# A two-layer streaming encoder step in split fp32: first stages reordered, low parts read last, and the order of norms, weight splits and down tiles moved

## The chip, the cores and the metric

The kernel runs on one core of a Trainium2 chip. The metric is the device time of one execution in microseconds (us). TensorE multiplies, ScalarE (ACT in the rows), VectorE (DVE) and GpSimd (POOL) do elementwise work, each from its own instruction stream, and SyncE (SP) issues most DMAs. The streams are synchronised by semaphores that the kernel writes out by hand.

## The reference

```python
def reference(x_prompt, x_sample, state_conv, cache_k, cache_v, ...):
    for i in range(2):
        hp, hs = rms_norm(xp, g_mix[i]), rms_norm(xs, g_mix[i])
        if i == 0:      # conformer convolution
            gp = conv_glu_in(hp, w_pw1[0], b_pw1[0])        # a * sigmoid(gate), 1024 -> 2 x 1024
            ...         # 31-tap depthwise conv, LayerNorm, silu, pointwise w_pw2
        else:           # 16 heads, 4 kv heads, window of own and 2 previous chunks of 64
            qp, kp, vp = qkv_proj(hp, w_qkv[0], qn_g[0], kn_g[0])
            mp = swa_prompt(qp, kp, vp, sinks[0], w_o[0])
            ...
        xp = xp + mp
        xp = xp + swiglu_ffn(rms_norm(xp, g_ffn[i]), w_gate[i], w_up[i], w_down[i])   # 2816 wide
        ...             # the same for xs
```
`xp` has 1024 rows and `xs` 32, of 1024 channels each. All data are float32.

## The kernel before

The residual `x` stays in SBUF for the whole step, channels on partitions (8 blocks of 128), tokens along the free dimension. The tokens are two halves: A is the first 512, B the other 512 and the 32 sample rows (544). A half is worked through a stage as a whole, then the other.

Every float32 product is made of three in the faster fp32r format. An operand is split into a high part, which ScalarE writes with a Copy into an fp32r tile, and a low part, the rest. A weight of 128x1024 comes by DMA into `raw`, ScalarE's `hi()` (L857) copies it to `whi`, GpSimd's `lo()` (L1909) subtracts to `wlo`. There are two buffers of each, used in turn; a program-wide list of tiles (`tags`) fixes which weight is n-th. For weight n, `hi()` waits for the DMA and, through `whi_free`, for the last product that reads `whi` of weight n-2; `lo()` waits for `hi()` and for the end of weight n-2's tile. The normalised half is split too, into `hAh` and `hAl` (or `hBh`, `hBl`): ScalarE writes the high part of a block of 128 channels, then VectorE the low part (`low`, L1406).

`proj` (L346, L355) makes one output tile of 128 channels: for each of 8 blocks high x high and high weight x low half, then `mid`, other TensorE work put between, then low weight x high half. A tile of the A half is 24 products of 512 columns in one PSUM bank, one of the B half 48 products of 272 columns in two banks. `take` hands out banks in two rings of four and makes TensorE wait until the last user of a bank has given it back.

The order of the work is written out by hand for each engine. First, x is transposed, its rows' factors are found by ScalarE, and A is normalised by products with diagonals (L427). `SEQ1` is then the order of 29 tiles of the first pointwise product (`g` is the gate, `a` the value). Each place in it is a slot, and ScalarE, VectorE and GpSimd have their share of the A half's convolution in each. Of 31 taps, VectorE adds most up in PSUM (`conv`, L1508), and `NP` of them ScalarE multiplies (`taps`, L987) and GpSimd adds (L1940). Then come the channel mean (L364), the mean of squares (L381), the norm `lnA`, the second pointwise product, and so on.

A feed-forward stage `ffn(l, h)` has 11 groups. Group G makes gate and up tiles of two blocks (b = 0 to 3) and then `down` (L560, L567) of group G-1: 8 output tiles d, of which the first four read one weight buffer (u = 0) and the last four the other (u = 1). VectorE's `add_to_x` (L1592) adds each to `x` and frees its bank. Six weights belong to a group, and `hi()` runs ahead of them: the four calls in b = 0 to 3 make those of b = 2, b = 3 and of `down`'s two halves, the fifth and sixth those of the next group's b = 0 and b = 1.

In the stages `ffn(0, "B")` and `ffn(1, "A")` the attention of the other half runs in the same groups. In group G VectorE reads the scores of four units of G-1 (`read_scores`), ScalarE takes their exps (`exps`, L1100), VectorE the reciprocals of their sums (`denominators`, L1656), ScalarE scales them (`scale_probs`, L1112). Group G+1 turns them and multiplies by the values, which ScalarE and VectorE split (`out_high`, L1069; `out_low`, L1680). `act_high` (L1059) and `act_low` (L1604) split the activation for the next group's `down`. VectorE's part behind the tiles of b is this:

```python
for d in range(KD):
    if G:
        add_to_x(("D", l, h, G - 1, d))
    if d == 1:
        read_scores(att, cur, 3)
    if d == 2:
        out_low(att, prev, 3)
    if d == 3:
        act_low(l, h, G, 1)
    if G and d % 2:
        denominators(att, cur, d // 2)
```

Of the kernel before, what the change touches and what calls it, by code (L numbers as in the profile page):

```python
# [38 lines left out]
NP = {"A": 10, "B": 10}  # L39
# [22 lines left out]

def conv_a_steps():

    done, glu, out = 0, 0, []
    for s in range(len(SEQ1)):
        if s and SEQ1[s - 1][:2] == ("a", "A"):
            glu += 1
        want = 0 if s < 2 else 1 if s in (5, 6) else 6 if s < 5 else 7
        new = KD * NQ["A"] if s == len(SEQ1) - 1 else done + want  # L70
        new = min(new, glu * NQ["A"])
        out.append((done, new))
        done = new
# [19 lines left out]
def products(h, j):  # L93

    return min(KD * NP[h], NP[h] * (j + 5) // NQ[h]) if j else 0

# [8 lines left out]
def build(nc, a, outs):  # L105
    y_prompt, y_sample, conv_prompt, conv_sample, k_prompt, v_prompt, k_sample, v_sample = outs
    with ExitStack() as ctx:
# [88 lines left out]
        late_in = sem("late_in")  # L196
        params_in, sinks_in, copied = sem("params_in"), sem("sinks_in"), sem("copied")
# [9 lines left out]
        row_sq, row_rs, diag_ready = sem("row_sq"), sem("row_rs"), sem("diag_ready")  # L207
# [25 lines left out]

        last_tile = {}
        w_need = {}
# [56 lines left out]
        def _(pe):  # L292
            user, used, to_free, nxt = [None] * 8, [0] * 8, [0] * 8, [0, 0]
# [3 lines left out]
            def take(key, h, ring=0):  # L297
                b = nxt[ring]
                if h == "B" and b % 2:
                    b += 1  # L300
                b %= 4
                w = CH[h]
                nxt[ring] = (b + w) % 4
                b += 4 * ring
# [32 lines left out]
            def proj(h, key, ev, n, last=True, mid=None):  # L337
                take(key, h)
                out = parts(key)
                pe.wait_ge(w_hi, n + 1)  # L340
                for k in range(KD):
                    if ev:
                        wait_h(h, ev, k)
                    for src in (hi_[h], lo_[h]):
                        for o, c0, w in out:
                            ins = nc.tensor.matmul(o, whi[n % 2][:, P * k:P * (k + 1)], src[:, k, c0:c0 + w],  # L346
                                                   start=(k == 0 and src is hi_[h]), stop=False)
                if last:
                    ins.then_inc(whi_free, 1)
# [3 lines left out]
                for k in range(KD):  # L353
                    for o, c0, w in out:
                        ins = nc.tensor.matmul(o, wlo[n % 2][:, P * k:P * (k + 1)], hi_[h][:, k, c0:c0 + w],  # L355
                                               start=False, stop=(k == KD - 1))
# [27 lines left out]
            def row_factors():  # L384

                b = take(("mean", "mix0B"), "B")
                for t in range(4, 9):
                    pe.wait_ge(diag_ready, t + 1)
# [5 lines left out]
            def x_group(q):  # L394
                t, half = q // 2, q % 2
                w = P if t < 8 else TS
                b = take(("xt", q), "A", int(q >= 8))
# [8 lines left out]
            pe.wait_ge(consts, 9)  # L406
            for q in range(8):
                x_group(q)
                if q == 5:
                    pe.wait_ge(params_in, 16 * 7)  # L410
                    b = take(("par", 0), "A", 1)
                    nc.tensor.transpose(ps[:, b, 0:40], R[0:40, 0:P], ident[0:40, 0:40])
                    for z in range(2):
                        ins = nc.tensor.transpose(ps[:, b, P + 120 * z:P + 120 * (z + 1)],
                                                  R[0:120, P * (3 + z):P * (4 + z)], ident[0:120, 0:120])
                    ins.then_inc(pfull[b], 1)
                    b = take(("par", 1), "A", 1)
                    for z in range(2):
                        ins = nc.tensor.transpose(ps[:, b, 124 * z:124 * (z + 1)], R[0:124, P * (1 + z):P * (2 + z)],
                                                  ident[0:124, 0:124])  # L420
                    ins.then_inc(pfull[b], 1)
# [1670 lines left out]
```

## Time and profile before

| | |
|---|---|
| median of 3 runs | 2288.69 us (2288.39 to 2290.41) |
| profiled execution, its own time | 2286.99 us |
| its span | 2285.2 us |
| busy share PE, PEld, DVE, ACT, POOL | 98%, 88%, 49%, 45%, 49% |
| granted TensorE clock, mean | 0.988 of full |
| HBM read, written | 184.39 MB, 5.10 MB |

The span runs from the first to the last instruction. PE is TensorE's products, PEld its weight loads. The chain of work that ended last lies on TensorE for 91% of the span. In a row of the timeline stand the start, the length, engine, line, operation, what is written and read, how many were merged, and in brackets the engine's idle time before it with what ended that.

### The profile page before, as it was taken

Reading aid. Unit: us, or ns where it says so; the run is one execution under the profiler, and the core shown is the slowest. Engines: PE = TensorE matmul, PEld = TensorE weight load, DVE = VectorE, ACT = ScalarE, POOL = GpSimd, SP = SyncE. Lnnn points to the kernel's source line nnn. Section 1 sums busy time; section 2 is a strip of 40 time slices with the busy share of each in tenths; the row PEclk is TensorE's granted clock in tenths of the full one; section 3 lists DMA queues with packets and bytes.
Section 4 is the critical chain, followed back from the end, with each engine's and each line's share of the span. In section 5 each row is a group of like instructions: output and inputs, shape, how many; then the busy total and the mean of one; then the engine's idle time right before and its main releaser. Section 6 shows DMA issues by size and latency. Waiting matters only on the chain.

```text
span 2285.2 us, 34556 instructions
## 1 busy us (share of the span) xinstructions
PE 2228.7 (98%) x13954; PEld 2017.0 (88%) x13954; DVE 1111.8 (49%) x1822; ACT 1037.8 (45%) x1659; POOL 1113.6 (49%) x573
## 2 busy tenths in 40 slices
PE   8998899999999999999999999999999999999999
PEld 7797678887889799999999898888888989999999
DVE  4987668873434544445443535454554142222223
ACT  6544655533524654544552466465655332222222
POOL 3787569975446533333334544333333443443433
PEclk9999899999999999999999999999999999999999
DMA  4111123332333522222222342222222323233222
GB/s 149 47 54 57 57 65 102 97 102 83 94 100 89 104 86 79 75 74 75 75 75 84 93 99 84 83 83 78 80 84 75 92 77 99 93 102 93 84 89 90
DMA packets 313644, 194.15 MB, mean 85 GB/s; under 512 B 40374, under 2 KB 286734, under 8 KB 313486
## 3 DMA queue, kind: packets, MB, share of 16 engines
q1 hardware_dynamic: 311608, 190.83, 28.3%
q8 instruction: 112, 1.84, 0.3%
q10 hardware_dynamic: 1878, 1.11, 0.2%
q14 instruction: 46, 0.38, 0.1%
HBM read 184.39 MB, written 5.10 MB: 83 GB/s over the span
## 4 chain that ended last, share of the span: by engine, by line
PE 91%; POOL 3%; DVE 2%; ACT 2%; issue 1%; DMA 0%; ACTq 0%; DVEq 0%; POOLq 0%
PE ps L346 42%; PE ps L355 21%; PE ps L560 14%; PE ps L567 7%; PE ps L530 2%; POOL accp L1940 2%; PE ps L516 1%; PE ps L364 1%; PE ps L492 1%; PE ps L491 1%; POOL wlo L1909 1%; PE ps L381 1%; DVE x L1592 1%; POOL rs L1919 0%; DVE sq L1401 0%
## 5 line engine op out<-in xcount | busy, mean ns | idle before, releaser
L1909 POOL TENSOR_TENSOR wlo<-raw,whi 128x1024 fp32r<-128x1024 f32 x342 | 838.9, 2453 | 1095.4 <-PE ps L355 763.7
L857 ACT ACTIVATE whi<-raw 128x1024 fp32r<-128x1024 f32 x342 | 361.8, 1058 | 628.4 <-PE ps L346 366.6
L346 PE MATMUL ps<-hBh,whi 128*128 128x272 f32 x2112 | 440.7, 290 | 6.0 <-DVE x L1592 3.2
L346 PE MATMUL ps<-hBl,whi 128*128 128x272 f32 x2112 | 440.0, 290 | 0.0
L346 PE MATMUL ps<-hAh,whi 128*128 128x512 f32 x1056 | 418.7, 397 | 18.5 <-DVE hAl L1406 10.5
L346 PE MATMUL ps<-hAl,whi 128*128 128x512 f32 x1056 | 416.1, 394 | 0.0
L1592 DVE TENSOR_TENSOR x<-ps,x 128x512 f32<-128x512 f32 (+1 forms) x368 | 258.4, 705 | 244.2 <-PE ps L567 181.3
L346 PEld LDWEIGHTS ps<-hBh,whi 128*128 128x128 f32 x2112 | 334.2, 190 | 8.9 <-issue 4.9
L346 PEld LDWEIGHTS ps<-hBl,whi 128*128 128x128 f32 x2112 | 332.4, 189 | 0.0
L355 PE MATMUL ps<-hBh,wlo 128*128 128x272 f32 x2112 | 291.2, 290 | 0.0
L355 PEld LDWEIGHTS ps<-hBh,wlo 128*128 128x128 f32 x2112 | 273.7, 188 | 2.5 <-issue 1.9
L355 PE MATMUL ps<-hAh,wlo 128*128 128x512 f32 x1056 | 270.6, 399 | 2.9 <-POOL wlo L1909 2.9
L346 PEld LDWEIGHTS ps<-hAh,whi 128*128 128x128 f32 x1056 | 200.3, 190 | 68.8 <-DVE hAl L1406 11.1
L1599 DVE TENSOR_TENSOR s<-ps,s 128x512 f32<-128x512 f32 (+1 forms) x88 | 62.3, 708 | 369.3 <-PE ps L355 367.2
L355 PEld LDWEIGHTS ps<-hAh,wlo 128*128 128x128 f32 x1056 | 197.0, 190 | 46.6 <-issue 4.3
L346 PEld LDWEIGHTS ps<-hAl,whi 128*128 128x128 f32 x1056 | 200.9, 190 | 40.8
L1940 POOL TENSOR_TENSOR accp<-accp,prod 128x512 f32<-128x512 f32 (+1 forms) x144 | 199.7, 1387 | 25.2 <-ACT prod L987 12.4
L1665 DVE TENSOR_TENSOR ptl<-ps,pth 128x512 fp32r<-128x512 f32 (+1 forms) x64 | 42.1, 658 | 167.1 <-ACT pth L1088 167.1
L1508 DVE SCALAR_TENSOR_TENSOR ps<-gxB,dwc,ps 128x574 f32<-128x574 f32 x152 | 114.1, 811 | 0.0
L1088 ACT ACTIVATE pth<-ps 128x512 fp32r<-128x512 f32 (+1 forms) x64 | 36.6, 572 | 167.6 <-PE ps L516 167.6
L1508 DVE SCALAR_TENSOR_TENSOR ps<-gxA,dwc,ps 128x512 f32<-128x512 f32 x152 | 101.8, 749 | 0.0
L560 PE MATMUL ps<-act0h,whi 128*128 128x272 f32 (+1 forms) x288 | 78.6, 327 | 4.5 <-DVE x L1592 3.9
(254 smaller groups left out, 3161.7 us busy)
## 6 DMA issues: line engine op xcount, KB each, us to landing
raw<-in_w_gate_dram SPq DMA_DIRECT2D x88, 512.0 KB, 3.8
raw<-in_w_up_dram SPq DMA_DIRECT2D x88, 512.0 KB, 3.8
raw<-in_w_down_dram SPq DMA_DIRECT2D x88, 512.0 KB, 3.6
raw<-in_w_pw_dram SPq DMA_DIRECT2D x38, 512.0 KB, 4.0
raw<-in_w_qkv_dram SPq DMA_DIRECT2D x32, 256.0 KB, 3.7
raw<-in_w_o_dram SPq DMA_DIRECT2D x64, 128.0 KB, 2.9
stage<-in_x_prompt_dram SPq DMA_DIRECT2D x8, 512.0 KB, 5.7
raw<-in_w_qkv_dram SPq DMA_DIRECT2D x8, 512.0 KB, 3.7
```

The lines of the kernel that those rows point to most:

```text
L346: ins = nc.tensor.matmul(o, whi[n % 2][:, P * k:P * (k + 1)], src[:, k, c0:c0 + w], start=(k == 0 and src is hi_[h]), stop=False)
L355: ins = nc.tensor.matmul(o, wlo[n % 2][:, P * k:P * (k + 1)], hi_[h][:, k, c0:c0 + w], start=False, stop=(k == KD - 1))
L530: ins = nc.tensor.matmul(ps[0:HD, 6, 0:256], v[:, slot, HD * g:HD * (g + 1)], p[:, 256 * z:256 * (z + 1)], start=(z == 0 and w == 0), stop ...
L560: ins = nc.tensor.matmul(o, whi[n % 2][:, wc], src[s + e][:, c0:c0 + w], start=(e == 0 and src is ach), stop=False)
L567: ins = nc.tensor.matmul(o, wlo[n % 2][:, wc], ach[s + e][:, c0:c0 + w], start=False, stop=(e == 1))
L857: nc.scalar.activation(whi[n % 2][:], raw[n % 2][:], ACT.Copy).then_inc(w_hi, 1)
L1508: link(nc.vector.scalar_tensor_tensor((X, Y)[q % 2], two(gx[h][:, c, t:t + w]), dwc[:, KD * t + c:KD * t + c + 1], (X, Y)[q % 2], ALU.mult ...
L1592: nc.vector.tensor_tensor(xd, pt(key), xd, ALU.add).then_inc(fr(key), 1)
L1599: nc.vector.tensor_tensor(s, pt(key), s, ALU.mult).then_inc(fr(key), 1)
L1665: nc.vector.tensor_tensor(ptl[:, 0:w], ps[:, 5, 0:w], f(pth[:, 0:w]), ALU.subtract).then_inc(pt_lo, 1)
L1909: nc.gpsimd.tensor_tensor(wlo[n % 2][:], raw[n % 2][:], f(whi[n % 2][:]), ALU.subtract).then_inc(w_lo, 1)
L1940: nc.gpsimd.tensor_tensor(accp[p % 2][:, 0:w], accp[p % 2][:, 0:w], prod[r % 2][:, 0:w], ALU.add).then_inc(padd, 1)
```

## The change

1. `NP["A"]` is 9 instead of 10, so VectorE has 24 steps for a channel block instead of 23. `conv_order` puts the last two steps of a block behind the first six of the next, which uses two other banks. `CONV_A` gives 8 steps to a slot instead of 7.
2. The opening: dummy products (`keep_busy`) before the transposes, before the normalising products and after the squares' mean of `lnA`. The gains come by their own semaphore, the other parameters are transposed later. The normalising products of blocks 2 to 7 stand inside the first tile (`ahead`). The x transposes of B use a ring of two banks. ScalarE writes the diagonals of B and loads the sigmoid table behind them.
3. `proj`: a tile that is the first to read a normalised half (`new`) goes through all high x high products, then low weight x high, then high weight x low. Its `whi` is free only at its end, so that `hi()` two weights later waits for the whole tile.
4. Norms: `factor` loads its table before it waits for the mean; the means of mix1B and ffn1B and some sums of squares of lnB have other places; in the last norm VectorE normalises ahead of its adds. The channel mean of A takes the last block straight from `gx`.
5. `ffn` on ScalarE, stages with attention: the fifth `hi()` of a group stands before `out_high` and `act_high`, the sixth before the last exps.

```diff
-NP = {"A": 10, "B": 10}
+NP = {"A": 9, "B": 10}
...
+def conv_order(h):
+    own = [[(p, q) for q in range(NQ[h])] for p in range(KD)]
+    if h == "B":
+        return sum(own, [])
+    out, ends = [], []
+    for p in range(KD):
+        out += own[p][:6] + ends + own[p][6:-2]
+        ends = own[p][-2:]
+    return out + ends
...
-        want = 0 if s < 2 else 1 if s in (5, 6) else 6 if s < 5 else 7
+        want = 0 if s < 2 else 2 if s in (5, 6) else 6 if s < 5 else 8
...
+def products_a(s):
+    return 0 if s < 2 else min(KD * NP["A"], 2 * (s - 1) if s < 6 else 8 + 3 * (s - 5))
...
+        RINGS = [(0, 4), (4, 4), (6, 2)]
...
+            def whi_done(ins, n):
+                whi_read[n] = len(whi_read) + 1
+                ins.then_inc(whi_free, 1)
...
+                new = ev and waited.get(h, 0) < h_need(ev, KD - 1)
...
                 for k in range(KD):
-                    if ev:
-                        wait_h(h, ev, k)
-                    for src in (hi_[h], lo_[h]):
...
+                    if ahead is not None:
+                        ahead(k)
+                    if k == 0:
+                        pe.wait_ge(w_hi, n + 1)
+                    if new:
+                        pe.wait_ge(h_hi[h], h_need(ev, k))
+                    ins = product(whi, hi_, k, start=(k == 0))
+                    if not new:
+                        ins = product(whi, lo_, k)
+                if not new and last:
+                    whi_done(ins, n)
...
+                if new:
+                    for k in range(KD):
+                        wait_h(h, ev, k)
+                        ins = product(whi, lo_, k, stop=(k == KD - 1))
...
+            def keep_busy(n):
+                for _ in range(n):
+                    nc.tensor.matmul(ps[:, 7, 0:P], ident[:], ones_d[:], start=True, stop=True)
...
+            keep_busy(10)
             for q in range(8):
                 x_group(q)
...
+            keep_busy(14)
+            half_a(0)
+            half_a(1)
...
-            pe.wait_ge(csummed, KD - 1)
-            mean(("lm", "A"), "A", ones_d, csum)
+            b = take(("lm", "A"), "A")
+            pe.wait_ge(csummed, KD - 2)
+            nc.tensor.matmul(ps[:, b, :], ones_d[:], csum[:, 0:512], start=True, stop=False)
+            pe.wait_ge(c_ready, KD)
+            nc.tensor.matmul(ps[:, b, :], ones_d[:], gx["A"][:, ORDER["A"][-1], 0:512], start=False, stop=True
+                             ).then_inc(pfull[b], 1)
             proj("B", ("a", "B", 1), "mix0", load(("a", 1)))
             square_mean("lnA", lambda k: pe.wait_ge(sq_ready, k + 1))
+            keep_busy(24)
...
-                         mid=(lambda: norm_mean("mix1B")) if (h, d) == ("A", 2) else None)
+                         ahead=(lambda k: k or norm_mean("mix1B")) if (h, d) == ("A", 3) else None)
...
-                        down(l, h, G - 1)
-                if (l, h) == (1, "A"):
-                    norm_mean("ffn1B")
+                        down(l, h, G - 1, (lambda: norm_mean("ffn1B")) if (l, h, G) == (1, "A", NG - 1) else None)
...
-                if n >= 2:
-                    act.wait_ge(whi_free, n - 1)
+                if n - 2 in whi_read:
+                    act.wait_ge(whi_free, whi_read[n - 2])
+                elif n >= 2:
+                    full(act, last_tile[n - 2])
...
+                nc.scalar.preload_act_table_set("natural_log_exp_and_others")
                 full(act, key)
...
-                nc.scalar.preload_act_table_set("natural_log_exp_and_others")
...
+                    first = att and G and (l, h, G) != (1, "A", NG - 1)
+                    if first:
+                        hi()
                     if att:
                         out_high(att, prev, 3)
                     act_high(l, h, G, 1, att)
...
                     if att:
                         exps(att, cur, 0)
                         exps(att, cur, 1)
-                    if G:
+                    if G and not first:
                         hi()
                     if att:
                         scale_probs(att, cur, 0)
                         exps(att, cur, 2)
                         scale_probs(att, cur, 1)
+                    if first:
+                        hi()
+                    if att:
                         exps(att, cur, 3)
-                    if G:
+                    if G and not first:
                         hi()
...
                 for d in range(KD):
-                    add_to_x(("D", l, h, NG - 1, d))
                     if (l, h) == (1, "A"):
...
                         norm_parts("ffn1B", C_FFN[1], d, d + 1)
+                    add_to_x(("D", l, h, NG - 1, d))
...
-                            if G == 6:
-                                for k in (2, 3):
-                                    sum_squares("lnB", k)
                         lo()
+                        if (l, h, G) == (0, "A", 6):
+                            for k in (2, 3):
+                                sum_squares("lnB", k)
```

## Rows read from the trace of the kernel before

**Rows 1.** The page, busy time and share of each engine.
```profile
PE 2228.7 (98%) x13954; PEld 2017.0 (88%) x13954; DVE 1111.8 (49%) x1822; ACT 1037.8 (45%) x1659; POOL 1113.6 (49%) x573
```

**Rows 2.** TensorE's waits: what for, us in total, times, longest.
```profile
PE ps L346 <- DVE hAl L1406: 10.5, 6, 7.1
PE ps L364 <- POOL csum L1962: 8.9, 1, 8.9
PE ps L346 <- ACT s L968: 4.8, 1, 4.8
...
PE ps L346 <- DVE x L1592: 4.0, 2, 3.2
PE ps L560 <- DVE x L1592: 3.9, 3, 1.3
PE ps L346 <- ACT qraw L1143: 3.7, 2, 1.9
...
PE ps L355 <- POOL wlo L1909: 2.9, 1, 2.9
```

**Rows 3.** Timeline of ScalarE in one group of the B half's stage.
```profile
949.67 0.38 ACT L1069 ACTIVATE hAh<-ps 64x256 fp32r<-64x256 f32 x1 [1.64 <-PE ps L530]
950.07 0.66 ACT L1059 ACTIVATE act3h<-s 128x544 fp32r<-128x544 f32 x1
950.75 1.28 ACT L1100 ACT_TABLE_LOAD   x1
952.04 0.41 ACT L1100 ACTIVATE sco<-sco,col 128x129 f32<-128x129 f32 x1
...
952.83 0.49 ACT L1100 ACTIVATE sco<-sco,col 128x257 f32<-128x257 f32 x1
...
955.24 1.06 ACT L857 ACTIVATE whi<-raw 128x1024 fp32r<-128x1024 f32 x1 [1.33 <-PE ps L560]
956.21 0.68 ACT L1112 ACTIVATE sco<-sco,col 128x128 f32<-128x128 f32 x2
```

**Rows 4.** Timeline of VectorE and of GpSimd in the same group.
```profile
954.60 0.16 DVE L1656 RECIPROCAL col<-col 128x2 f32<-128x2 f32 x1
954.68 0.70 DVE L1592 TENSOR_TENSOR x<-ps,x 128x544 f32<-128x544 f32 x1
...
956.50 2.85 DVE L1604 TENSOR_TENSOR act3l<-s,act3h 128x544 fp32r<-128x544 f32 x1
...
956.38 2.39 POOL L1909 TENSOR_TENSOR wlo<-raw,whi 128x1024 fp32r<-128x1024 f32 x1 [4.90 <-ACT whi L857]
```

**Rows 5.** Timeline of TensorE in the same group: ends and starts of tiles.
```profile
954.73 0.41 PE L560 MATMUL ps<-act1l,whi 128*128 128x272 f32 x2
...
955.64 0.49 PE L560 MATMUL ps<-act0h,whi 128*128 128x272 f32 x2
...
960.20 0.49 PE L560 MATMUL ps<-act0h,whi 128*128 128x272 f32 x2 [1.31 <-DVE x L1592]
```

**Rows 6.** Timeline of one group of layer 1's A half: ScalarE, VectorE, TensorE.
```profile
1528.98 1.06 ACT L857 ACTIVATE whi<-raw 128x1024 fp32r<-128x1024 f32 x1 [0.73 <-PE ps L560]
...
1528.57 0.67 DVE L1592 TENSOR_TENSOR x<-ps,x 128x512 f32<-128x512 f32 x1
...
1527.80 0.40 PE L560 MATMUL ps<-act0h,whi 128*128 128x512 f32 x1
```

**Rows 7.** Stretches: us, PE, PEld, DVE, ACT, POOL busy, granted clock, DMA.
```profile
83.12:205.27 122.15, 122.15 (x817) 114.27 (x815) 110.08 (x176) 62.00 (x86) 108.62 (x77) 1.00 0.17 50
...
214.00:219.00 5.00, 4.84 (x17) 3.81 (x18) 2.66 (x5) 1.94 (x4) 2.41 (x2) 0.55 0.25 74
536.60:546.60 10.00, 7.12 (x26) 5.46 (x25) 3.21 (x5) 3.26 (x5) 8.38 (x5) 0.83 0.19 52
767.90:773.20 5.30, 5.26 (x16) 4.22 (x17) 2.14 (x4) 0.53 (x2) 0.65 (x1) 0.68 1.08 187
1348.90:1353.00 4.10, 4.06 (x32) 4.09 (x33) 2.01 (x3) 1.09 (x4) 0.76 (x1) 1.00 0.99 206
```

More of the change, by code:

```diff
@@ L60, with joined @@
 GLU = [(h, c) for w, h, c in SEQ1 if w == "a"]
+def conv_order(h):
[7 more added lines that the diff above has]
+    return out + ends
+CONV = {h: conv_order(h) for h in "AB"}
+def joined(h, j):
+    return sum(q == NQ[h] - 1 for _, q in CONV[h][:j])
 def conv_a_steps():
@@ L297, in take @@
             def take(key, h, ring=0):
+                first, size = RINGS[ring]
                 b = nxt[ring]
@@ L353, in proj @@
                 for k in range(KD):
-                    for o, c0, w in out:
-                        ins = nc.tensor.matmul(o, wlo[n % 2][:, P * k:P * (k + 1)], hi_[h][:, k, c0:c0 + w],
-                                               start=False, stop=(k == KD - 1))
+                    ins = product(wlo, hi_, k, stop=(not new and k == KD - 1))
+                if new:
+                    for k in range(KD):
+                        wait_h(h, ev, k)
+                        ins = product(whi, lo_, k, stop=(k == KD - 1))
                 ins.then_inc(pfull[place[key][0]], 1)
@@ L396, in x_group @@
                 w = P if t < 8 else TS
-                b = take(("xt", q), "A", int(q >= 8))
+                b = take(("xt", q), "A", 2 if q >= 8 else 0)
                 if half == 0:
@@ L542, in values, with down @@
                 ins.then_inc(pv_full, 1)
-            def down(l, h, G):
+            def down(l, h, G, between=None):
                 stage_ft = FT * (2 * l + (h == "B"))
@@ L547, in down @@
                 for u in range(2):
+                    if u and between is not None:
+                        between()
                     n = load(("D", l, G, u))
@@ L971, in _, with taps @@
             done = {"A": 0, "B": 0}
-            def taps(h, j):
-                for i in range(done[h], products(h, j)):
+            def taps(h, n):
+                for i in range(done[h], n):
                     p, c, t, r = in_order(h, i)
@@ L1002, in _ @@
                     row_factor(4, 9)
+                    act.wait_ge(row_rs, 4)
+                    nc.scalar.activation(rsc[:, 4:9], rsc[:, 4:9], ACT.Copy, scale=float(D)).then_inc(row_rs, 1)
+                    act.wait_ge(row_rs, 5)
+                    for t in range(4, 9):
+                        w = P if t < 8 else TS
+                        nc.scalar.activation(diag[0:w, t, 0:w], ident[0:w, 0:w], ACT.Copy, scale=rsc[0:w, t:t + 1]
+                                             ).then_inc(diag_b, 1)
+                    nc.scalar.preload_act_table_set("sigmoid_and_others")
                 if s == 5:
@@ L1415, in norm_parts, with x_copy @@
                         low(ev[-1], ev[:-1], k)
-            for q in range(8):
+            def x_copy(q):
                 full(dve, ("xt", q))
@@ L1447, in late_params @@
             def late_params():
+                full(dve, ("par", 1))
+                b = place["par", 1][0]
+                nc.vector.tensor_copy(stc[:], ps[:, b, 248:488])
+                nc.vector.tensor_copy(dwc[:], ps[:, b, 0:TAPS * KD]).then_inc(fr(("par", 1)), 1)
                 full(dve, ("par", 2))
@@ L1498, in conv @@
                             freed(dve, ("par", 1))
[L1499 to L1502 removed]
+                        if h == "A" and p < 2:
+                            for key in before_conv[2 * p:2 * p + 2]:
+                                freed(dve, key)
+                    if q == (0 if h == "A" else 1) and pos:
+                        dve.wait_ge(c_ready, pos - 1 if h == "A" else pos)
                     if q < 2:
@@ L1929, in _, with taps @@
             summed = {"A": 0, "B": 0}
-            def taps(h, j):
-                for i in range(done[h], products(h, j)):
+            def taps(h, n):
+                for i in range(done[h], n):
                     p, c, t, r = in_order(h, i)
```

178 lines of the change are left out of this document (90 added, 88 removed).

## The prediction

> **What bounds the kernel now.** I read the page's busy shares first: TensorE is busy 98% of the span [rows 1], so nothing can win much: the idle time, 2285.2 - 2228.7 = 56 us over the whole span, and some half-rate clock. It can lose more, by making TensorE wait where it doesn't now. The list of TensorE's waits shows where the idle time lies [rows 2]: 10.5 us for the low parts of a normalised half, 8.9 us for the last channel sum of the convolution, 4.8 us for a sigmoid, 2.9 us for one weight low part, and small ones for PSUM banks that VectorE's adds or ScalarE's copies give back. None lies in the two long attention-and-feed-forward stages but three gaps of 1.3 us. Last I read those stages engine by engine, since the change moves a waiting instruction there: ScalarE [rows 3, 6], VectorE and GpSimd [rows 4], TensorE [rows 5, 6]. What the reader is to see there: inside `down` of the B half TensorE fills two pairs of banks in turn, so tile d starts only after VectorE's `add_to_x` of tile d-2. Tile 4 starts at 955.64, right behind the add of tile 2 (954.68 + 0.70) [rows 4, 5]. That add stands on VectorE behind the reciprocal at 954.60, which waits for `exps(0)` on ScalarE. So the chain ScalarE exps, VectorE reciprocal, VectorE add, TensorE tile has no slack already.
>
> **The step that decides: the early `hi()`.** Of the six weight copies in a group the fifth is that for the next group's first tile. It reuses the buffer that `down`'s first half reads, so it waits for that half's last hi/lo product whatever its place: 954.73 + 0.41 = 955.14, and the copy starts at 955.24 [rows 3, 5]. Before, `out_high`, `act_high`, a table load and four exps ran ahead of it, from 949.67 to 953.8. The change puts it ahead of them all (`first`). It can't start earlier, and what stands behind it on ScalarE now waits from 948 to 955. That ScalarE lets nothing pass is in the rows: the probabilities' scaling had its reciprocal at 954.76, but ran at 956.21, after the copy [rows 3, 4]. The Trainium skill ("TensorE: Matmul & The Clock Gate", "Architectural detail: the array is 16× 32×32, not 1× 128×128") says of ScalarE and VectorE that their queues are strictly first in, first out; by a queue that could pass, the step would cost nothing (the first rival), and the row sides with the page.
>
> New chain in the B-half stage, from the copy's start: copy 0.97, `out_high` 0.40, `act_high` 0.68, table load 1.29, first exps 0.79 and its read 0.1 [rows 3]: 955.24 + 4.2 = 959.5. Reciprocal 0.08, add 0.70: 960.3; TensorE picks up 0.2 later, 960.5 instead of 955.64 [rows 4, 5]. That is 4.8 us for each group with scores to turn, which are groups 1 to 8. Three of these groups have today a gap of 1.3 us (1.4 with its restart), because `act_low` took 2.85 us beside GpSimd's weight split [rows 2, 4, 5]. There `act_low` now comes at 961.4, after that split has ended (956.38 + 2.39), and I take the gap as gone. 5 x 4.8 + 3 x 3.4 = 34 us. The Trainium skill ("SBUF — State Buffer", "SBUF: two separate sides") says that VectorE with two SBUF inputs and GpSimd exclude each other for a whole instruction; this agrees with the 2.85 us. If the gap stayed all the same, the sum would be 4 us higher. Groups 9 and 10 have no scores, but `out_low` and `act_low` still wait for the late `out_high` and `act_high`: about 1.5 us each (0 if VectorE catches up, 3 if `act_low` meets the split), 3 us. So 37 us in this stage.
>
> In the A-half stage of layer 1 a tile takes one bank of four, so tile 6 is the one that needs the add of tile 2. Copy at 1528.98 [rows 6], + 0.97 + 0.40 + 0.65 + 1.29 + 1.0 (two exps of 0.49) = 1533.3, add until 1534.0, TensorE at 1534.2. Tile 3 starts at 1527.80 and a tile takes 1.39, so tile 6 was due at 1532.0: 2.2 us, in groups 1 to 9: 20 us.
>
> **What the stalls do to the clock.** After the gap of 2.88 us 10 us ran at a granted 0.83, after that of 1.89 us 5.3 us at 0.68, each 1.7 us of full clock lost; after 1.79 us it stayed at 1.00 [rows 7] (half rate is 1.2 GHz, full 2.4). A gap of 4.8 us in otherwise dense work should cost it each time: 8 x 1.6 = 13 us. Gaps of 2.2 us lie between the row that fell and those around it; I take two in three, 9 x 2/3 x 1.6 = 10 us. Bounds for both together: 0 and 27.
>
> **What it wins.** First stages: the ends of `conv` are spread (8 steps a slot instead of 7, so that the last slot has 2 instead of 17), the last channel goes straight to TensorE, and the wait of 8.9 us should fall to some 1.5. The 4.8 us wait for the sigmoid falls to about 1: three products fewer stand ahead, and its table (1.29 us) is loaded before. Half rate around 214 us (5 us at 0.55) gives back 2.2 and that after the sigmoid's wait 1.5 [rows 2, 7]. The opening, where the first tile is threaded between the normalising products, wins some 3 us, but x transposes on two banks instead of four then wait for ScalarE, about 1.5 to 2 back. Against it, VectorE: it was busy 110.1 of 122.2 us [rows 7], and 20 more steps of 0.67 make it 123.5, so it lags by 1 to 3 us. Extra dummy products cost 0 to 2 (ahead of the diagonals, else in idle time). Together 15 us, bounds 5 and 20. For these dummy products no row of before exists; the nearest are the normalising ones.
>
> Low parts last: at lnA the first hi comes 2 us earlier (table loads moved), but TensorE is then idle most of the time until the eighth, so its remaining 16 products may run at half rate: 1 us won, bounds -1.5 and 3. ffn0A the same way 1 (bounds 0 and 3). The other norms had no such wait; there the copy for the next but one tile waits for the whole tile, 2 us later, covered by a tile of 5.4 or 6 us. lnB: `sum_squares` 2 and 3 move behind the weight split that TensorE waited 2.9 us for; with 1.4 of clock 4.3. ffn0B and ffn1A: table load ahead of the wait, 1.3 each of the two `qraw` waits of 1.89 and 1.79, and 1.7 of clock: 4.3. mix1B's mean one tile later 1.5. ffn1B: mean half a `down` earlier, norm ahead of the adds, lows last: the 3.2 us wait becomes about 1, and the tile gets denser: 4 (bounds 2 and 5). Sum of gains 15 + 1 + 1 + 4.3 + 4.3 + 1.5 + 4 = 31.
>
> **Sum.** 37 + 20 + 13 + 10 - 31 = +49 us. The profiled execution took 2286.99 us (span 2285.2 and 1.8 around it), 1.7 below the median of the runs; so 2336 in the profile and about 2337 as a median. I state 2337.
>
> **Rivals.** (1) Faster: the moved copy costs nothing, as it would if ScalarE's work behind it were not needed before 961. For it: ScalarE waits for TensorE for that copy today too. Against it: tile 4's start at 955.64 hangs on the exps. It decides if the first exps of a group end within 0.2 us of today's 952.9. Then only the gains are left: 2257; with a stall under 1 us a group still faster. Chance 0.12. (2) The stalls come, but the clock doesn't fall for them: + 57 - 31, 2314. For it: the gap of 1.79 us. Against it: the 1.89 and the 2.88. Chance 0.18. (3) VectorE becomes the bound of the first convolution, the dummy products and low clock eat the rest there, and the first stages win under 5 us: 2347. For it: 123.5 us of work in 122.2. Against it: TensorE's banks allow a lag of one tile. Chance 0.12. (4) No net change, stalls half as long and just paid by the gains: 0.02. My forecast: 0.56.
>
> **Numbers.** Measured noise of this kernel is about 0.2% (4.6 us). Faster 0.12, same 0.02, slower 0.86. The range takes in forecast, (2) and (3) with the bounds of the gains and of the clock: 2300 to 2354; it leaves out (1) and (4) and a little on the far side.
>
> **What would show it.** In the profile after: ScalarE's copy of a group standing before `act_high` and waiting some 7 us for TensorE; TensorE waits at `down` for VectorE's add, 8 of 4 to 5 us and 9 of about 2, and the clock under 1 behind them. In the first 220 us: the channel-mean product at about 201 instead of 214, VectorE near full. If ScalarE's exps still end before `down`'s fourth tile, the main step is wrong; if the gaps are there and the clock row stays at 1.00, (2) holds.

## The result, and the profile after

The kernel after takes 2352.73 us (median of four runs, 2351.52 to 2355.49), the one before, on the same chip, 2288.89 (2288.39 to 2290.41): ratio 1.0279, 95% interval 1.0262 to 1.0297, or 64 us slower. 2337 was predicted, with a range to 2354. The profiled execution of after took 2355.49 us (span 2353.6), 2.8 above its median. It has a stretch of half rate near 30 us, and its first 230 us took 3.3 us longer than those of the first experiment, whose order is the same there and whose profile has no such stretch.

TensorE's waits of after (what for, us in total, times, longest), to be held against [rows 2]:
```profile
PE ps L640 <- DVE x L1686: 60.1, 21, 5.0
PE ps L387 <- issue: 8.8, 2, 4.5
PE ps L387 <- ACT hAh L988: 4.6, 6, 1.0
PE ps L387 <- ACT s L1050: 4.0, 2, 3.2
PE ps L387 <- ACT hAh L975: 3.1, 3, 1.5
PE ps L387 <- ACT qraw L1234: 3.1, 2, 1.7
```
One row has taken over: TensorE in `down` waits 60.1 us, 21 times, for VectorE's `add_to_x` (L1686), where it was 3.9 us in 3. The waits for the channel sum (8.9) and for a weight's low part (2.9) are gone. Two of 4.5 and 4.3 us "issue" are new, before the first tile of the B half in the first convolution and in the last norm; both are taken up below. The second was 3.2 us before and then had the name `DVE x`.

The same group of the B half's stage as in [rows 3 to 5], ScalarE, VectorE, TensorE:
```profile
957.19 1.06 ACT L937 ACTIVATE whi<-raw 128x1024 fp32r<-128x1024 f32 x1 [7.21 <-PE ps L640]
958.27 0.38 ACT L1160 ACTIVATE hAh<-ps 64x256 fp32r<-64x256 f32 x1
958.67 0.66 ACT L1150 ACTIVATE act3h<-s 128x544 fp32r<-128x544 f32 x1
959.35 1.28 ACT L1191 ACT_TABLE_LOAD   x1
960.64 0.40 ACT L1191 ACTIVATE sco<-sco,col 128x129 f32<-128x129 f32 x1
...
961.55 0.17 DVE L1750 RECIPROCAL col<-col 128x2 f32<-128x2 f32 x1 [4.92 <-ACT sco L1191]
961.63 0.70 DVE L1686 TENSOR_TENSOR x<-ps,x 128x544 f32<-128x544 f32 x1
...
963.46 0.71 DVE L1698 TENSOR_TENSOR act3l<-s,act3h 128x544 fp32r<-128x544 f32 x1
...
957.18 0.41 PE L647 MATMUL ps<-act1h,wlo 128*128 128x272 f32 x2
962.60 0.79 PE L640 MATMUL ps<-act0h,whi 128*128 128x272 f32 x2 [5.00 <-DVE x L1686]
```
Read it downwards: the copy stands first and waits 7.21 us for TensorE's last read of the old weight. Everything else of ScalarE follows it, the exps end where the reciprocal can start at 961.55, the add follows, and TensorE, which had nothing more to do at 957.6, goes on at 962.60. From copy to reciprocal it is 4.36 us. `act_low` takes 0.71 where it took 2.85 beside the weight split.

A group of layer 1's A half, for [rows 6]:
```profile
1531.88 1.06 ACT L937 ACTIVATE whi<-raw 128x1024 fp32r<-128x1024 f32 x1 [6.60 <-PE ps L640]
...
1536.25 0.67 DVE L1686 TENSOR_TENSOR x<-ps,x 128x512 f32<-128x512 f32 x1
...
1536.97 0.50 PE L640 MATMUL ps<-act2h,whi 128*128 128x512 f32 x1 [1.96 <-DVE x L1686]
```

Stretches of after (columns as in [rows 7]): the first convolution, the two norms of A, lnB's first tile, a feed-forward tile that waited for `qraw`, the products behind one stall of each stage, and behind the gap of the last norm:
```profile
83.00:206.00 123.00, 120.57 (x784) 112.94 (x785) 122.03 (x193) 62.03 (x87) 109.09 (x78) 0.97 0.17 47
226.00:248.00 22.00, 17.37 (x73) 12.81 (x73) 12.54 (x19) 14.68 (x21) 0.90 (x1) 0.77 0.00 1
300.00:316.00 16.00, 12.89 (x53) 9.76 (x53) 15.80 (x25) 7.64 (x12) 5.37 (x4) 0.79 0.22 62
536.00:546.00 10.00, 10.00 (x46) 8.29 (x45) 1.56 (x2) 5.27 (x8) 9.71 (x7) 1.00 0.21 60
757.00:762.00 5.00, 3.32 (x15) 2.42 (x14) 2.14 (x4) 2.73 (x6) 2.37 (x1) 1.00 1.08 210
961.30:968.30 7.00, 5.70 (x25) 5.74 (x26) 3.37 (x7) 3.68 (x14) 0.00 (x0) 0.52 0.28 77
1538.40:1541.90 3.50, 3.50 (x10) 2.68 (x10) 2.65 (x7) 2.79 (x9) 0.34 (x1) 0.51 0.02 7
1941.00:1945.00 4.00, 3.74 (x17) 3.77 (x18) 3.91 (x7) 2.26 (x3) 0.14 (x1) 0.57 0.00 0
```
VectorE is now busy 122.03 of 123 us in the first convolution (110.08 of 122.15 before), and behind a stall of 5.0 us, as behind one of 1.96, TensorE runs near half of its 2.4 GHz.

To see where the time goes, the start of one and the same TensorE product is read in both traces, and their distances are subtracted. For the norms that product is the start of the third tile behind them. The -5.3 of the first stages holds the 3.3 us of the half rate near 30 us. The right column does this for the first experiment, which takes the early copies out:

| stretch, ends at | predicted | after - before | first experiment - before |
|---|---|---|---|
| first stages (squares' mean, 223.15 before) | -15 | -5.3 | -8.6 |
| lnA | -1 | +0.5 | +0.2 |
| ffn0A | -1 | +0.9 | +0.8 |
| lnB | -4.3 | -4.7 | -4.7 |
| ffn0B, ffn1A, mix1B (tables, mean) | -5.8 | -2.4 | -2.2 |
| early copies, B half's stage | +50 | +51.5 | 0 |
| early copies, A half's stage | +30 | +27 | 0 |
| last norm (ffn1B) | -4 | +0.9 | +0.7 |
| sum | +49 | +68.4 | -13.8 |

### The profile page after: what moved, and what is told of

It reads as the page before. It is cut to its first block, busy times and chain, and to the rows that moved or that the text cites. A ratio compares the mean times of both kernels' runs of the same rounds, so it can differ in the third digit from the quotient of the medians.

```text
span 2353.6 us, 34735 instructions
## 1 busy us (share of the span) xinstructions
PE 2258.1 (96%) x14052; PEld 2043.4 (87%) x14052; DVE 1112.4 (47%) x1825; ACT 1032.2 (44%) x1657; POOL 1100.0 (47%) x564
## 4 chain that ended last, share of the span: by engine, by line
PE 91%; ACT 5%; DVE 3%; issue 1%; POOL 0%; DVEq 0%; ACTq 0%; POOLq 0%
PE ps L387 64%; PE ps L640 14%; PE ps L647 6%; PE ps L608 2%; PE ps L594 1%; PE ps L419 1%; ACT L1191 1%; ACT whi L937 1%; ACT sco L1191 1%; DVE x L1686 1%; PE ps L569 1%; PE ps L570 1%; PE ps L436 1%; DVE sq L1498 1%; PE ps L464 0%
## 5 line engine op out<-in xcount | busy, mean ns | idle before, releaser
L387 PE MATMUL ps<-hBh,whi 128*128 128x272 f32 x2112 | 435.4, 290 | 11.1 <-issue 8.8
L387 PE MATMUL ps<-hBl,whi 128*128 128x272 f32 x2112 | 432.3, 289 | 0.0
L387 PE MATMUL ps<-hAh,whi 128*128 128x512 f32 x1056 | 416.4, 397 | 13.8 <-ACT hAh L988 4.6
L387 PE MATMUL ps<-hAl,whi 128*128 128x512 f32 x1056 | 409.8, 394 | 0.0
L1686 DVE TENSOR_TENSOR x<-ps,x 128x512 f32<-128x512 f32 (+1 forms) x368 | 257.2, 704 | 244.7 <-PE ps L647 185.9
L387 PEld LDWEIGHTS ps<-hAl,whi 128*128 128x128 f32 x1056 | 201.0, 190 | 42.3
L2034 POOL TENSOR_TENSOR accp<-accp,prod 128x574 f32<-128x574 f32 (+1 forms) x136 | 189.9, 1397 | 31.3 <-ACT prod L1069 19.9
L1605 DVE SCALAR_TENSOR_TENSOR ps<-gxA,dwc,ps 128x512 f32<-128x512 f32 x160 | 107.2, 748 | 0.0
L1179 ACT ACTIVATE pth<-ps 128x512 fp32r<-128x512 f32 (+1 forms) x64 | 36.6, 572 | 156.0 <-PE ps L594 156.0
```

What stands on the lines that cost most here:

```text
L387: ins = nc.tensor.matmul(o, wt[n % 2][:, P * k:P * (k + 1)], src[h][:, k, c0:c0 + w], start=start, stop=stop)
L1605: link(nc.vector.scalar_tensor_tensor((X, Y)[q % 2], two(gx[h][:, c, t:t + w]), dwc[:, KD * t + c:KD * t + c + 1], (X, Y)[q % 2], ALU.mult ...
L1686: nc.vector.tensor_tensor(xd, pt(key), xd, ALU.add).then_inc(fr(key), 1)
L2034: nc.gpsimd.tensor_tensor(accp[p % 2][:, 0:w], accp[p % 2][:, 0:w], prod[r % 2][:, 0:w], ALU.add).then_inc(padd, 1)
```

## The experiments

### Is it the moved copies, and which of them

The first kernel puts both early `hi()` back and keeps all the rest of the change; the second does the opposite, the kernel before with the early copies alone; the third has only the sixth copy early.
```diff
-                    first = att and G and (l, h, G) != (1, "A", NG - 1)
-                    if first:
-                        hi()
...
-                    if G and not first:
+                    if G:
                         hi()
                     if att:
                         scale_probs(att, cur, 0)
```


> The changed kernel with the fifth and sixth weight copies of a group back in their old places, all else as changed. Theory (the early fifth copy costs both attention stages): the 51.5 and 28.8 us that the two stages lost come back, so about 2272 us, faster than before by some 16 us, with no gap over 2 us at down in these stages. Rival (the longer stages come from the low parts read last or from a buffer that is freed later): 2300 us or more, and gaps remain.

Measured: 2274.03 us (2272.88 to 2275.84), ratio 0.9934, interval 0.9919 to 0.9949. TensorE's wait in `down` is back at its old size:
```profile
PE ps L387 <- issue: 8.8, 2, 4.4
PE ps L387 <- ACT hAh L988: 4.6, 6, 1.0
PE ps L640 <- DVE x L1681: 4.6, 4, 1.3
PE ps L387 <- ACT s L1050: 4.0, 2, 3.2
```


> The kernel before with only the two copies moved ahead. Theory: eight gaps of 4.7 to 5.0 us in the B half's stage, nine of 1.7 to 2.2 us in the A half's, half-rate clock behind them, together about 80 us: 2369 us. Rival (the stalls need the other edits too): under 2330 us.

Measured: 2368.93 us, ratio 1.0343, interval 1.0326 to 1.0361; the wait for the add is 59.6 us in 20 times.

> The changed kernel with the fifth copy back in its place and the sixth still ahead of the last exps. Theory (the fifth alone does it): within 5 us of the kernel with both back, about 2272 us. Rival (both share the loss, since the last exps then wait for the end of down): 2290 to 2320 us.

Measured: 2276.69 us, ratio 0.9944, interval 0.9929 to 0.9959. The profile has none of the stalls.

So the change is two things that hardly touch each other: the early copies cost 2352.7 - 2274.0 = 78.7 us on top of the rest, and 3.4%, about 79, on top of the kernel before; the rest wins 15.3, against the kernel before run beside it (2289.30). Of the copies it is the fifth. The sixth, put before the last exps, reads 2.7 us more, with overlapping intervals.

### What part of a stall is clock

Eighteen dummy products for TensorE before the second half of `down`, in the B half's stage of after, for each of its eight long stalls (`G` in the edit is that of `down`, 0 to 7, so these are groups 1 to 8). They stand where TensorE has nothing to do, and write to a bank that nobody reads.
```diff
                     if u and between is not None:
                         between()
+                    if u and (l, h) == (0, "B") and G <= 7:
+                        keep_busy(18)
```


> The changed kernel with 18 dummy products (3.9 us at full rate) put into each of the eight waits of 4.7 to 5.0 us in the B half's stage; results unchanged. Theory (the wait costs twice, once as idle time and once as half rate behind it): the clock stays at full, and 8 x 1.6 = 13 us come back: about 2340 us. Rival (behind the wait VectorE's adds pace the tiles, so the half rate costs nothing): 2350 us or more.

Measured: 2340.93 us, ratio 1.0225, interval 1.021 to 1.024: 11.8 us less than after. The same group in its trace, TensorE (the row of the dummies counts two records for each):
```profile
953.65 4.18 PE L464 MATMUL ps<-ones_d,ident 128*128 128x128 f32 x36
958.82 0.49 PE L642 MATMUL ps<-act0h,whi 128*128 128x272 f32 x2 [0.99 <-DVE x L1688]
959.15 0.41 PE L642 MATMUL ps<-act0l,whi 128*128 128x272 f32 x2
```
The add still comes when it came, so the stall is as long; but two products behind it take 0.41 us at once, where in after the next ones took 0.66. This is the clock's share, apart from that of the wait. From trace to trace the stage is 14.4 us shorter than in after, and 37.1 us longer than before; after's own profiled run lay 2.8 above its median, so the medians show 11.8.

The change's own dummy products (`keep_busy(10)`, `(14)`, `(24)`) removed from the first experiment:
```diff
-            keep_busy(10)
...
-            keep_busy(14)
...
-            keep_busy(24)
```


> The changed kernel with the copies back and without any of the 48 dummy products. Theory (they warm the clock for the opening's transposes, but their 14 in the middle delay the normalising products by about 1 us, and the 24 at lnA only move the half-rate stretch): within 3 us of 2274 us. Rival (they keep the clock where it counts): 2278 us or more.

Measured: 2273.71 us (2272.09 to 2277.98), ratio 0.9934, interval 0.9921 to 0.9948, so no difference to 2274.03.

### Where the gains of the first stages went

All kernels from here on have the copies back. The first puts the normalising products of blocks 2 to 7 into the other ring, because the second tile had stood 3.2 us for the first one's sigmoid:
```diff
-                b = take(("xn", k), "A", 1 - k % 2)
+                b = take(("xn", k), "A", 1 - k % 2 if k < 2 else 1)
```


> The changed kernel with the copies back, and the normalising products that stand inside the first tile take banks of the other ring, so that the second tile no longer takes the first tile's bank and doesn't wait for its sigmoid. Theory (the opening's gain was lost to this bank): the wait of 3.2 us before the second tile goes, 1 to 2 of it come back as a later wait for the x transposes' copies, so about 2 us faster than with the copies back alone, some 2272 us. Rival (VectorE sets when the first B tile's pair is done, whatever the opening): no change there, 2274 us.

Measured: 2271.73 us (2269.97 to 2272.18), ratio 0.9921, interval 0.9907 to 0.9934, 2.3 us less. The wait for the first sigmoid is gone; a wait of 1.3 us for ScalarE's copy of an x transpose has come at 33.7 us, as the theory had it.

Then every tile takes its blocks in pairs, high and low, as before the change, instead of the lows last:
```diff
-                new = ev and waited.get(h, 0) < h_need(ev, KD - 1)
+                new = False
...
-                    if new:
-                        pe.wait_ge(h_hi[h], h_need(ev, k))
+                    if ev:
+                        wait_h(h, ev, k)
```


> The changed kernel with the copies back, and no tile takes the low parts last: each block waits for its low part and takes high and low in pairs, as before. Theory (after the last high part comes TensorE still has two thirds of the tile to do, at half rate, so reading lows last wins next to nothing): within 3 us of 2274 us, half-rate stretches of the same length at lnA. Rival (lows last wins 1 to 2 us at each of lnA, ffn0A and ffn1B): 2277 to 2280 us.

Measured: 2267.56 us, ratio 0.9903, interval 0.9889 to 0.9916: 6.5 us less than 2274.03. Neither theory had it; the lows-last order, taken for a small gain, costs. Stretches of the first experiment (lnA's and ffn0A's first tiles), then of this one:
```profile
220.00:245.00 25.00, 20.36 (x89) 14.90 (x88) 13.11 (x20) 16.32 (x23) 1.48 (x1) 0.80 0.04 12
290.00:312.00 22.00, 19.02 (x96) 15.14 (x95) 19.02 (x27) 11.19 (x16) 7.35 (x5) 0.84 0.13 38
```
```profile
220.00:245.00 25.00, 21.35 (x95) 15.68 (x95) 15.96 (x24) 18.79 (x26) 5.91 (x4) 0.86 0.08 22
290.00:312.00 22.00, 19.38 (x101) 15.56 (x100) 19.23 (x27) 14.64 (x20) 10.76 (x7) 1.00 0.16 48
```
Both the number of products left and their clock differ. Lows last, TensorE does eight single products, at lnA 1.4 us apart as ScalarE brings the blocks, and then sixteen at once, most of them at half rate; in pairs the second product of a block fills part of each wait and fewer are left. From the start of the last block's first product to the end of the tile there are 17 products against 10, a difference of 1.6 us at full rate; it is 6.4 us against 4.1 at lnA and 5.9 against 2.4 at ffn0A, where no half rate is left with pairs. From start of lnA's first tile to that of its third it is 20.9 us with the lows last (226.71 to 247.57) and 19.3 in pairs (224.33 to 243.64); in ffn0A 17.4 (299.13 to 316.53) and 14.7 (295.20 to 309.91), of which 1.4 is given back in the groups behind. The opening gives 1.8, since a low-last tile frees `whi` only at its end and the copy, a table load and the sigmoid come behind that (the second tile's wait is 0.8 us with pairs, 3.2 without); the first convolution gives 0.6 and layer 1 1.8.

Both together:

> The copies back, every tile taking its blocks high and low in pairs, and the normalising products of blocks 2 to 7 in the other ring of banks. Paired alone had brought 2267.6 and the other ring alone 2271.7, against 2274.0 with neither. Theory: the ring removes the second tile's wait for the first one's sigmoid and the pairing what the late low parts cost at lnA, ffn0A and the two qkv halves, so they add up, but both take from the wait before the second tile (3.2 us, 0.8 left with the pairing), so their sum of 8.7 loses about 1: 2266, and no half rate before 80 us. Rival: the time from the second tile to the first B tile is set by VectorE, and what the ring gives is waited for again before the first B tile: within 1 of 2267.6.

Measured: 2267.14 us (2266.04 to 2268.15), ratio 0.9903, interval 0.9886 to 0.9919. The rival: the first B tile starts 1.3 us sooner than with the pairing alone (79.56 for 80.90), and at lnA only 0.75 us are left of it.

In all these kernels TensorE stands 4.4 us before its first B tile. The row says "issue", so the profile names no releaser; the bank that the tile takes is that of A's fourth gate tile, whose sigmoid in after ran from 84.66 to 85.33, behind ScalarE's high parts of the norm of B and three convolution products, and TensorE went on at 85.43. This kernel puts that sigmoid into ScalarE's idle time behind the fifth high part:
```diff
                     for k in range(4 * (s - 5), 4 * (s - 4)):
                         n_hi_part("mix0B", k)
+                        if k == 4:
+                            sigmoid(sig)
+                            sig += 1
```


> The kernel before it (i) with ScalarE's sigmoid of the fourth gate tile of A put behind the fifth high part of the norm of B, in idle time, instead of behind the eighth and three convolution products. Theory: the 4.4 us that TensorE stands before its first B tile are a wait for the bank which that sigmoid frees; with it early the low parts of B (the last at about 80.8 in the kernel with the copies back) are only needed at 81, so the gap falls under 1 and its half-rate stretch goes: 5 to 6 us less than i, about 2260. Rival: VectorE is the bound of the whole stretch; TensorE then waits elsewhere before 210 us, for a bank of a gate or value tile, and i's time stays within 1.5 us.

Measured: 2266.15 us (2265.47 to 2266.81), ratio 0.9897, interval 0.9882 to 0.9912: within 1 us of the kernel without it. TensorE starts its first B tile without a wait, and then:
```profile
85.82 0.82 PE L387 MATMUL ps<-hBh,whi 128*128 128x272 f32 x2 [4.26 <-DVE gxA L1566]
```
The wait has moved by one tile and now carries its real name: VectorE's value tile. That is the rival, VectorE as the bound.

Last, four of VectorE's convolution steps moved out of the two slots in which it also normalises B (with the sooner last norm of the next section):
```diff
-        want = 0 if s < 2 else 2 if s in (5, 6) else 6 if s < 5 else 8
+        want = 0 if s < 2 or s in (5, 6) else 6 if s < 5 else 8
```


> Kernel k and the sooner last norm of m together, and VectorE's four convolution steps of the two slots in which it also normalises B (slots 5 and 6, two each) moved to the slots behind them, with 8 in each as before and fewer left for the last. In k the gap of 4.3 us had only moved to the second B tile, where it was a wait for VectorE's value tile (gxA), with VectorE busy without a break before it. Theory: VectorE is the bound only in the slots with the norm; four steps of 0.68 us less there bring that value 2.7 us earlier, the gap falls to 1.6 and its half-rate stretch of 3.4 us (1.7 of full clock) goes: 4 us less, with 1 from m 2261 to 2262. Rival: VectorE is the bound of the whole convolution (121 us busy of 125); the four steps are then waited for at the channel mean near 203 us, 2 to 3 us, and the time is within 1 of 2265.

Measured: 2263.78 us (2263.10 to 2264.93), ratio 0.9886, interval 0.987 to 0.9903, the fastest of all. TensorE, two places of its trace, and the stretch:
```profile
84.36 0.52 PE L387 MATMUL ps<-hBh,whi 128*128 128x272 f32 x2 [1.86 <-DVE gxA L1568]
...
204.03 1.12 PE L530 MATMUL ps<-gxA,ones_d 128*128 128x512 f32 x2 [2.11 <-DVE gxA L1619]
...
80.00:205.00 125.00, 121.02 (x793) 111.57 (x793) 122.86 (x195) 60.99 (x85) 110.61 (x78) 1.00 0.18 52
```
Both theories are half right. The gap fell by 2.4 us as expected and its half rate went. But the steps taken away are asked for at the channel mean: 2.11 us that weren't there. VectorE, 122.86 of 125 us busy, is the bound of the whole stretch. The two waits together fell from 4.26 to 3.97 us and the squares' mean came 1.2 us sooner than in the kernel before this one, so what was won there is mostly the clock.

### The last norm

The old order of ffn1B in the first experiment (mean behind the whole `down` of group 9, adds ahead of the norm):
```diff
-                        norm_parts("ffn1B", C_FFN[1], d, d + 1)
                     add_to_x(("D", l, h, NG - 1, d))
+                    if (l, h) == (1, "A"):
...
+                        norm_parts("ffn1B", C_FFN[1], d, d + 1)
```


> The changed kernel with the copies back and the last norm (ffn1B) as before: mean behind the ninth down, adds ahead of the norm's steps; lows still last. Theory (the new order keeps back the add that frees the first B tile's banks, so an earlier mean wins nothing): the wait before the first B tile is shorter than 4.3 us, about 3, and from the start of the tenth group's downs to the third B tile no more than 42.3 us pass. Rival (the new order wins, but less than the 4 us of the forecast): over 43 us pass.

Measured, a single run: 2278.59 us. From the start of `down` of group 9 to the third B tile it is 43.65 us, not 42.3 or less; 42.03 in the first experiment, 41.35 before. TensorE:
```profile
1860.75 1.85 PE L387 MATMUL ps<-hBh,whi 128*128 128x272 f32 x12 [3.00 <-issue]
1864.83 0.52 PE L387 MATMUL ps<-hBh,whi 128*128 128x272 f32 x2 [2.23 <-ACT hBh L977]
1866.12 0.59 PE L387 MATMUL ps<-hBh,whi 128*128 128x272 f32 x2 [0.77 <-ACT hBh L977]
```
So the old order needs the pairs to be good; with the lows last the tile runs into the high parts. The fourth case is in the kernel with pairs and the new order: 42.24 us. With pairs the old order is 0.9 us better than the new, with the lows last 1.6 worse.

The other way, in the kernel with both (2267.14): VectorE normalises two blocks between the ninth group's last adds, where it idles 0.7 us each time.
```diff
                         if G:
                             add_to_x(("D", l, h, G - 1, d))
+                        if (l, h, G) == (1, "A", NG - 1) and d in (5, 6):
+                            ...
+                            x_norm("ffn1B", d - 5, C_FFN[1])
```


> Kernel i with the last norm begun sooner: VectorE normalises its first two blocks between the last three adds of the ninth group's down, where it idles 0.7 us before each add, instead of behind them all. Theory: the gap of 4.3 us before the first B tile of the last stage is a wait for the bank that VectorE's sixth add frees, and that add is late because all eight blocks of the norm stand in between; two products of 0.78 us taken out ahead, one of which had met GpSimd's weight split and taken 2.2, bring the add 1.5 to 3 us earlier: 2 to 3 us less than i. Rival: the norm's own length beside the two splits decides wherever it begins, or the low parts are then the last wait: within 1 us of i.

Measured: 2266.38 us (2266.08 to 2267.06), ratio 0.9898, interval 0.9884 to 0.9913: the rival, within 1 us. TensorE still waits 4.36 us. VectorE in its trace:
```profile
1838.37 2.71 DVE L1502 TENSOR_TENSOR hBl<-sq,hBh 128x544 fp32r<-128x544 f32 x1
...
1845.63 2.73 DVE L1497 SCALAR_TENSOR_TENSOR sq<-x,col,rs 128x544 f32<-128x544 f32 x1
...
1851.02 0.68 DVE L1685 TENSOR_TENSOR x<-ps,x 128x512 f32<-128x512 f32 x1
```
One instruction of the norm meets each of GpSimd's two weight splits and takes 2.7 us for 0.75, whichever comes then; the add that frees the bank, the last row, ends at 1851.7, 0.1 before TensorE goes on.

## Why the prediction was right where it was, and where not

**The deciding step held.** Copy, `out_high`, `act_high`, table, exps, reciprocal: predicted 4.2 us from copy to reciprocal, 4.36 measured. The eight stalls were 4.5 to 5.0 us (38.4 together), groups 9 and 10 added 2.7, and the three old gaps of 1.3 are gone, as the 2.85 us of `act_low` are: 38.4 + 2.7 - 3.9 = 37.2 against 37. The A half's nine stalls were 1.7 to 2.2 us, 18.3 together for 20. That it is this step is shown, from both sides, by the first two experiments. The range held by little: 2352.73 lies 1.3 us under its upper end, with gains half as large as forecast and that of ffn1B outside its own bounds. That the time stayed inside was luck in part.

**The clock.** In the B half's stage 51.5 - 37.2 = 14.3 us are left for it, 13 were predicted, and the dummies in the stall won 14.4 of the stage: with them it costs 37.1 us over before, about the waits alone. In the A half's stage 27 - 18.3 = 8.7, against 10. Here not six but four of nine stalls were followed by half rate, 3.4 us each. Held against before group by group, each stall cost 0.27 us more than its idle time even where the clock stayed at 1.00, and those four a further 1.6 each: 9 x 0.27 + 4 x 1.6 = 8.8. The prediction had the clock alone. Where the 0.27 comes from no run shows.

**The first stages: 15 predicted, 5.3 and 8.6 measured.** This is one of the mis-sized terms. 3.3 us lie between the two measured values, those of the half rate near 30 us. Its parts: the wait for the channel sum went wholly (8.9, more than assumed) and the sigmoid's fell from 4.8 to 0.8, as forecast. But "the opening wins some 3 us" was wrong. The threaded products take their banks behind the first tile, so the second tile gets the first one's bank and stands 3.2 us for its sigmoid. And "it lags by 1 to 3 us" for VectorE was too small at one place: it also normalises B there, one step of that took 2.92 us beside a weight split, and the first B tile stood 4.4 us and TensorE's clock fell to half for 3.4 to 6.8 us. So the channel mean's product came at 210.1 us (206.8 in the first experiment) and not near 201. Rival (3) had the mechanism: VectorE is the bound of this stretch. The last experiments showed it, by a wait that moved from the bank to the value tile and then to the channel mean. Its price was near too, under 5 us of gain; that the time came out above its 2347 as well is due to the next points.

**Low parts last: +1 +1 and part of 4 predicted, a loss of about 6.5 in all.** This is a gain with the wrong sign. The prediction saw that "its remaining 16 products may run at half rate" and still took a gain. It had asked when the first product can start. What counts is how many products are left when the last block arrives, and at which clock they run. The experiment with pairs showed it, against both of its own expectations. With pairs the stages do win over before, 1.3 us at lnA and 0.7 at ffn0A with its groups, close to the 1 + 1 that was put down to the lows. The prediction had also taken the later copy at the other norms for "covered by a tile of 5.4 or 6 us"; it named no cost in the opening and in layer 1, and 1.8 us lie in each.

**ffn1B: a gain of 4 predicted, a loss of 0.9.** "The 3.2 us wait becomes about 1" looked to the norm and the low parts. TensorE already waited for a bank before, the one that the sixth add frees; VectorE in before:
```profile
1870.96 0.68 DVE L1592 TENSOR_TENSOR x<-ps,x 128x512 f32<-128x512 f32 x1
```
This add ends at 1871.64, and TensorE goes on at 1871.74. The new order puts six blocks of the norm ahead of that add instead of five, and two of its instructions meet splits (2.23 and 2.70 us); the bank is waited for 4.3 us.

**Tables and means.** lnB won 4.7 (4.3 predicted). The two `qraw` waits fell by 0.2 and 0.4 us only, not 1.3 each; the half rate behind the first of them went, as forecast. ScalarE in the trace of before, then of after:
```profile
762.93 1.06 ACT L857 ACTIVATE whi<-raw 128x1024 fp32r<-128x1024 f32 x1 [1.41 <-PE ps L346]
764.22 1.28 ACT L881 ACT_TABLE_LOAD   x1 [0.23 <-PE ps L364]
```
```profile
754.47 1.06 ACT L937 ACTIVATE whi<-raw 128x1024 fp32r<-128x1024 f32 x1 [1.41 <-PE ps L387]
755.54 1.28 ACT L956 ACT_TABLE_LOAD   x1
```
The load stood behind a weight copy that itself waits for TensorE, and had waited only 0.23 us for the mean; more was not to be won by putting it ahead of that. mix1B's mean no longer waits (1.15 us before), but a wait of 1.5 us for VectorE's scores came in the first group of layer 1's A half; it is not there in the kernels with pairs.

The sum: 79 for the early copies, where 80 were predicted; 15 won, where 31 were predicted. The difference of 16 is nearly the whole miss of the stated time.

## What to carry to other kernels

Before an instruction that waits is moved ahead on an engine, add up what then stands behind it and ask which other engine's next step hangs on that: here a copy that could start no sooner held 4.3 us of work. When a gap vanishes, look one tile further: if it comes back under another name, an engine's total is the bound, and only work taken off that engine helps. And a new order of products at a start should be judged by what is left when the last operand arrives.

## What the runs showed of the hardware

With each of after's eight stalls of 4.5 to 5 us inside dense products came 3.4 or 6.8 us in which the granted clock was 0.5; it began between 3.1 us before TensorE went on (1156.2, for 1159.3) and 0.7 us behind that (866.1, for 865.4). Of the A half's nine stalls the four of 1.95 us were followed by 3.4 us of it, the three of 2.23 us were not. In the kernel with dummies in the other stage the same nine stalls had it the other way: the three of 2.23 us and the last of 2.06 were followed by it, the four of 1.95 were not. So the length of a stall of this size doesn't decide. The gaps of 1.3 us in `down` and that of 1.7 us at 755.6 us in the first experiment left the clock at 1.00. A gap of 3.2 us in the opening came with half rate in the profiled execution of after (29.8 to 36.6 us) and of three of the experiments, and not in that of the first experiment, nor in that of the kernel without dummies, with the same gap. Dummy products in the eight stalls kept the clock at 1.00; the change's 48, in the opening and before lnA, were worth nothing.

VectorE instructions of 0.7 to 0.8 us with two inputs in SBUF (a block of the norm, its low part, `act_low`) took 2.2 to 2.9 us when they met GpSimd's weight split. The adds to `x`, which read one of their two inputs from PSUM, did not: all 98 that began inside a split in after took 0.68 to 0.73 us. The Trainium skill ("SBUF — State Buffer", "SBUF: two separate sides") says that a VectorE instruction with two SBUF inputs and a GpSimd instruction that reads SBUF exclude each other for a whole instruction; the rows at 1838.37 and 1845.63 and the adds agree.
